# Starting offsets of SBUF buffers: low weights, mixing operands and large buffers placed within 256 bytes

## What is computed

```python
for l in range(2):
    x = x + 0.5 * swiglu(rmsnorm(x, ln_ffn1[l]), w_ffn1_gu[l], w_ffn1_down[l])
    h = rmsnorm(x, ln_mix[l])
    u_pool, q, k, v, gate_logits = split(h @ w_in[l])
    a = pool_mixer(u_pool, pool_w[l], pool_scale[l]) @ w_pool_branch[l]
    b = swa_sink_attention(rope(rmsnorm(q)), rope(rmsnorm(k)), v, sinks[l]) @ w_attn_branch[l]
    g_pool, g_attn = split(sigmoid(gate_logits))
    x = x + (g_pool * a + g_attn * b) @ w_out[l]
    x = x + 0.5 * swiglu(rmsnorm(x, ln_ffn2[l]), w_ffn2_gu[l], w_ffn2_down[l])
p = rmsnorm(x) @ w_in_2
x = x + concat(gated_delta_rule_both_ways(p), mlstm_both_ways(p)) @ w_out_2
x = x + peer(rmsnorm(x))     # top 16 of 128 x 128 experts in 8 heads, tables u and v
return rmsnorm(x)
```

## Time and profile before

| | |
|---|---|
| median of 3 runs | 4139.93 us (4137.62 to 4139.94) |
| profiled execution | 4135.88 us, span 4134.0 us |
| TensorE matmuls | busy 4077.5 us, 99% of the span, 19348 of them |
| weight loads | busy 3377.9 us (82%), beside the matmuls |
| VectorE, ScalarE, POOL | 48%, 35%, 46% busy |
| DMA | 486.47 MB, mean 118 GB/s |
| granted TensorE clock | 0.997 |

### The profile page before, as it was taken

How to read it: one execution, slowest core, us unless ns; L and a number is a source line. 1 busy time by engine, 2 the same in 40 slices (tenths; PEclk the granted TensorE clock), 3 DMA queues, 4 the chain that set the end, 5 groups by cost and what they waited for, 6 DMA issues and landing times.

```text
span 4134.0 us, 52711 instructions
## 1 busy us (share of the span) xinstructions
PE 4077.5 (99%) x19348; PEld 3377.9 (82%) x19348; DVE 1981.6 (48%) x3472; ACT 1455.7 (35%) x2192; POOL 1884.1 (46%) x1408
## 2 busy tenths in 40 slices
PE   9999999999999999999999999999999999999998
PEld 7888777888888877888777998888888888888887
DVE  3212553221220364321248453498788846666653
ACT  3222243222322234322324433333676632222222
POOL 4444334444444434444433534455433345555553
PEclk9999999999999999999999999999999999999999
DMA  3222122222222212222211002233455575555542
GB/s 133 100 101 95 72 72 92 91 102 91 94 99 102 93 63 82 92 91 102 98 72 41 1 11 103 94 144 132 174 205 204 203 249 185 191 203 193 185 170 82
DMA packets 134660, 486.47 MB, mean 118 GB/s; under 512 B 8704, under 2 KB 74496, under 8 KB 92032
## 3 DMA queue, kind: packets, MB, share of 16 engines
q1 hardware_dynamic: 49392, 351.29, 23.7%
q10 hardware_dynamic: 85136, 133.38, 9.3%
HBM read 417.54 MB, written 67.11 MB: 117 GB/s over the span
## 4 chain that ended last, share of the span: by engine, by line
PE 43%; issue 32%; POOL 21%; DVE 2%; ACT 1%; POOLq 0%; ACTq 0%; DVEq 0%
POOL w_lo L446 21%; PE bank L1139 12%; PE bank L1140 12%; PE bank L1141 12%; PE bank L1961 1%; PE bank L1714 1%; PE bank L1730 1%; PE bank L1726 1%; DVE gk L2374 0%; DVE gq L2374 0%; PE bank L1896 0%; DVE p_t L2385 0%; PE bank L1675 0%; PE bank L1573 0%; DVE p_t L2388 0%
## 5 line engine op out<-in xcount | busy, mean ns | idle before, releaser
L446 POOL TENSOR_TENSOR w_lo<-raw,w_hi 128x512 fp32r<-128x512 f32 x1324 | 1784.1, 1379 | 2118.5 <-ACT w_hi L554 2091.8
L1139 PE MATMUL bank<-h_hi,w_hi 128*128 128x512 f32 x3232 | 1271.6, 393 | 20.0 <-DVE h_lo L2088 9.8
L1140 PE MATMUL bank<-h_lo,w_hi 128*128 128x512 f32 x3232 | 1260.5, 390 | 0.0
L1141 PE MATMUL bank<-h_hi,w_lo 128*128 128x512 f32 x3232 | 1260.2, 390 | 0.0
L554 ACT ACTIVATE w_hi<-raw 128x2048 fp32r<-128x2048 f32 x331 | 633.1, 1913 | 1051.7 <-PE bank L1141 1017.9
L1139 PEld LDWEIGHTS bank<-h_hi,w_hi 128*128 128x128 f32 x3232 | 608.4, 188 | 152.3 <-POOL w_lo L446 16.3
L1141 PEld LDWEIGHTS bank<-h_hi,w_lo 128*128 128x128 f32 x3232 | 607.8, 188 | 128.2
L1140 PEld LDWEIGHTS bank<-h_lo,w_hi 128*128 128x128 f32 x3232 | 608.5, 188 | 123.7 <-issue 1.5
L1139 PE MATMUL bank<-w_mix_hi,w_hi 128*128 128x512 f32 x1024 | 398.4, 389 | 0.9 <-ACT stage L942 0.9
L1141 PE MATMUL bank<-w_mix_hi,w_lo 128*128 128x512 f32 x1024 | 398.3, 389 | 0.0
L1140 PE MATMUL bank<-w_mix_lo,w_hi 128*128 128x512 f32 x1024 | 398.3, 389 | 0.0
(11 more groups left out here) (378 smaller groups left out, 4463.4 us busy)
## 6 DMA issues: line engine op xcount, KB each, us to landing
raw<-weights SPq DMA_DIRECT2D x331, 1024.0 KB, 4.8
g_store<-g_buf ACTq DMA_DIRECT2D x8, 4096.0 KB, 18.2
g_in<-g_store ACTq DMA_DIRECT2D x32, 1024.0 KB, 5.5
s_store<-stage ACTq DMA_DIRECT2D x60, 512.0 KB, 2.9
s_in<-s_store ACTq DMA_DIRECT2D x30, 1024.0 KB, 7.5
x<-x_in SPq DMA_DIRECT2D x4, 512.0 KB, 8.0
out<-x SPq DMA_DIRECT2D x8, 256.0 KB, 2.2
keys_sb<-keys ACTq DMA_DIRECT2D x1, 1024.0 KB, 4.7
```

The costliest lines, as they stand in the source:

```text
L446: pool.tensor_tensor(w_lo[:, slot, cols], raw[:, slot, cols], w_hi[:, slot, cols].bitcast(F32), ALU.subtract).then_inc(lo_written, 1)
L1139: pe.matmul(out_ap, w_hi[:, slot, cols], m_hi, start=start, stop=False)
L1140: pe.matmul(out_ap, w_hi[:, slot, cols], m_lo, start=False, stop=False)
L1141: return pe.matmul(out_ap, w_lo[:, slot, cols], m_hi, start=False, stop=stop)
```

## The change

place gets an argument shift. A buffer of 2048 bytes a partition or more now begins at a multiple of LINE = 256 bytes plus shift, a smaller one at a multiple of 32 as before. Low weights are shifted by 64, att, y and mix_late by 64, y2 by 192; all other large buffers begin at 0 modulo 256. soft and headsel are placed earlier, among the small buffers, and a few buffers that lie over others are computed to the same rule. What moves, modulo 256: w_lo and a_t from 0 to 64; att, y and mix_late from 128 to 64; qk, v_tok, gates, pool_w_sb from 128 to 0; y2 from 224 to 192; const and the buffers of the delta rule and the mLSTM from 224 to 0, gv from 96 to 0. w_hi, raw, h, act, w_mix, hot_first and hot_parts stay at 0; act and w_mix move by 256 bytes. The highest byte used becomes 212,704. No instruction, wait or transfer is added or removed.

```diff
--- before.py
+++ after.py
@@ -114,6 +114,8 @@
 
 GATE_STEP = {"rows": 1, "read": 2, "logs": 3, "a": 4, "sums": 5, "m": 7, "floor": 8}
 
+LINE = 256
+
 
 def build(nc, x_in, weights, gains, small, pool_w, consts, rope, second, level_masks,
           keys, out):
@@ -123,11 +125,12 @@
         sizes = {F32: 4, F32R: 4, U32: 4}
         offset = [0]
 
-        def place(name, shape, dtype, at=None):
+        def place(name, shape, dtype, at=None, shift=0):
 
             nbytes = int(np.prod(shape[1:])) * sizes[dtype]
             if at is None:
-                at = offset[0]
+                step = LINE if nbytes >= 2048 else 32
+                at = -(-(offset[0] - shift) // step) * step + shift
                 offset[0] = -(-(at + nbytes) // 32) * 32
             return nc.alloc_sbuf_tensor_at(name, shape, dtype, offset=at + base)
 
@@ -147,20 +150,21 @@
         raw = place("raw", [P, 2, TILE * P], F32)
         w_hi_at = offset[0]
         w_hi = place("w_hi", [P, 2, TILE * P], F32R)
-        w_lo_at = offset[0]
-        w_lo = place("w_lo", [P, 2, TILE * P], F32R)
+        w_lo_at = offset[0] + LINE // 4
+        w_lo = place("w_lo", [P, 2, TILE * P], F32R, shift=LINE // 4)
+        soft = place("soft", [P, 2, 6, 4], F32)
         rstd = place("rstd", [P, TOKENS], F32)
-        sq_at = offset[0]
+        sq_at = -(-offset[0] // LINE) * LINE
         sq = place("sq", [P, 2, TOKENS], F32)
-        tmp_at = offset[0]
+        tmp_at = -(-offset[0] // LINE) * LINE
         tmp = place("tmp", [P, TOKENS], F32)
         rcol = place("rcol", [P, 3, TT], F32)
         gain = place("gain", [P, 9, KB], F32)
         small_sb = place("small_sb", [P, LAYERS, 14], F32)
+        headsel = place("headsel", [P, 2], F32)
         const = place("const", [P, 5, P], F32)
         mask = place("mask", [P, 2 * P], F32)
         invc = place("invc", [P, 4, PAD], F32)
-        headsel = place("headsel", [P, 2], F32)
         rope_sb = place("rope_sb", [P, 2, TOKENS], F32)
         region = offset[0]
         ident, swap, upper, lower, ones = (const[:, n, :] for n in range(5))
@@ -185,14 +189,13 @@
         probs_t0 = place("probs_t0", [P, 2, TOKENS], F32)
         gates = place("gates", [P, 2 * KB, TOKENS], F32)
 
-        mix_late = place("mix_late", [P, 4, 2, TOKENS], F32R, at=offset[0] - KB * TOKENS * 4)
-        att_hi = place("att_hi", [P, 4, TOKENS], F32R)
-        att_lo = place("att_lo", [P, 4, TOKENS], F32R)
-        y_hi = place("y_hi", [P, 4, TOKENS], F32R)
-        y_lo = place("y_lo", [P, 4, TOKENS], F32R)
+        mix_late = place("mix_late", [P, 4, 2, TOKENS], F32R, at=offset[0] + LINE // 4 - KB * TOKENS * 4)
+        att_hi = place("att_hi", [P, 4, TOKENS], F32R, shift=LINE // 4)
+        att_lo = place("att_lo", [P, 4, TOKENS], F32R, shift=LINE // 4)
+        y_hi = place("y_hi", [P, 4, TOKENS], F32R, shift=LINE // 4)
+        y_lo = place("y_lo", [P, 4, TOKENS], F32R, shift=LINE // 4)
         pool_w_sb = place("pool_w_sb", [P, 4, P], F32)
         rq = place("rq", [P, 3, TT, 10], F32)
-        soft = place("soft", [P, 2, 6, 4], F32)
 
 
         offset[0] = region
@@ -215,8 +218,9 @@
         head_gain = place("head_gain", [P, 8], F32)
         r3 = place("r3", [P, 3, TT, 8], F32)
         rn = place("rn", [P, 3, 32], F32)
-        m_row_at = offset[0]
-        m_row = place("m_row", [GH, 2, TOKENS], F32)
+        m_row_at = -(-offset[0] // LINE) * LINE
+        m_row = place("m_row", [GH, 2, TOKENS], F32, at=m_row_at)
+        offset[0] = m_row_at + 2 * TOKENS * 4
         head_squares = place("head_squares", [P, GH * P], F32, at=m_row_at)
         masks2 = place("masks2", [P, 9, P], F32)
         sq_second = place("sq_second", [P, KB, TOKENS], F32, at=offset[0])
@@ -256,8 +260,8 @@
                for p in range(2)]
         state = place("state", [P, 2, GH, P], F32, at=region - 2 * GH * P * 4)
         offset[0] = overlay
-        y2_hi = place("y2_hi", [P, KB, TOKENS], F32R)
-        y2_lo = place("y2_lo", [P, KB, TOKENS], F32R)
+        y2_hi = place("y2_hi", [P, KB, TOKENS], F32R, shift=3 * LINE // 4)
+        y2_lo = place("y2_lo", [P, KB, TOKENS], F32R, shift=3 * LINE // 4)
         a_row = tmp
```

## The result

The changed kernel takes **4192.74 us** (median of 4 runs, 4191.86 to 4193.27) against 4138.77 for the kernel before on the same chip, a ratio of 1.0133 [1.0121, 1.0146]. It is 54 us slower; the forecast was 4085, 54 us faster. The profiled run took 4193.27 us with a span of 4191.4, 57.4 us more than the 4134.0 of the earlier trace rows.

What follows compares the result with a forecast made beforehand. It took TensorE's matmul pace to bound the kernel. From the profiled 4135.9 us it took 50 for the low weights and 5 for mixing operands and y2, giving 4081, then 4 more for the runs' median: 4085, range 4036 to 4168.

Steps and rivals of the forecast that it cites:

- What bounds the kernel: TensorE, busy 4077.5 of 4134.0 us: only a change in the pace of its matmul stream can move the time much.
- Part 1: Low weights to 64, in 4960 triples with h, act and w_mix: 10 ns less each, 50 us gained.
- What is lost at the best place: Matmul stream with operands at 0: 12 to 13 ns lost at the start of each matmul, whatever its length.
- Part 2: Mixing operands from 128 to 64, y2 from 224 to 192, 960 matmuls: 5 us less.
- Part 3: Everything else to 0, touching two-pass matmuls, vector and POOL work: no change in time.
- Part 4: POOL writing low weights at 64: its work stays covered, 7.4 us beside 10.7 us of matmuls.
- Rival A: Low weights at 64 break the stream's even beat in each triple: 4165, or 4214 if whole triples slow; chance 0.2.
- Rival B: Weight loads stay hidden, so moving low weights does nothing; 0 to 6 us gained elsewhere, 4134 to 4140; chance 0.12.
- Rival C: The matmul after the changed load speeds up too: 20 to 25 ns a triple, 4036 down to 4011; chance 0.1.

Runs made afterwards that it cites:

- experiment 7: Separate program, not the kernel: 24 matmul stretches at varied widths and modes; for 512 columns float32r 226.7 ns, plain float32 215 a record, bf16 216.
- experiment 5: The changed kernel with low weights, mixing operands and y2 all at 0: 4133.61 us, ratio 0.9991 to the kernel before.
- experiment 2: The changed kernel with only the low weights back at 0: 4133.41 us, ratio 0.9991 to the kernel before.
- experiment 1: The kernel before with only the low weights moved to 64: 4193.67 us, ratio 1.014.
- the map: Separate program: 120 stretches of 20 float32r triples at varied operand and weight places, later 63 more in finer steps; fastest 680.0 ns a triple.

## Why the prediction was wrong

**What bounds the kernel** held: the time moved only through the pace of the matmul stream, and the 57.4 us are all in TensorE's busy time.

**Part 1, low weights at 64, failed**, in sign. It took a gain of 10 ns for each of 4960 triples from L1379 as the only row with the weights 64 ahead of the moving operand. Two things were wrong with that row. First, it is not at 64: a row of pool_u is PAD + TOKENS = 528 values, 2112 bytes, so only the first of its four products begins at 64, the others at 128, 192 and 0. The four, with weights at 128 each time, leave eight records, two a product and not one:

```profile
449.35 3.67 PE L1379 MATMUL bank<-pool_u,pool_w_sb 128*128 128x512 f32 x8 [0.41 <-issue]
```

From the second record on they start 429 or 430 ns apart, at all four distances; and L1311, 96 bytes apart, keeps the same step (its three records of the earlier trace rows in 1.45 us are two steps of 429 and one duration of 592). Second, L1379 is plain float32, and experiment 7 shows 215 ns a pass for that at no distance at all: what the row lacks, the mode lacks. The working named this ("it may be the two passes that hide the cost") and went by the distance all the same. Four rows of the same mode as the stream, 233 at 128, 233.5 at 224, 231.7 with 32 columns and 0.40 beside weights at 224, had all pointed to a loss. The last of them holds: with everything at 0 (experiment 5) the matmul in front of L1311's load has 389 ns where it had 396. The nearest row had to be chosen by mode first. Instead of -10 the term is +13.3 ns where the stream is dense and +10.7 in the mean for h. The upper bound of the term, +6 for one matmul, was also too low, because it priced only the matmul beside the load.

**What is lost at the best place** is 13.3 ns in float32r at 512 and 256 columns, as read, but not "whatever its length": experiment 7 has 16.7 at 504 and 58 at 128.

**Part 2** was right in sign and near in size: 5 us expected, about 3 found at the 2.4 GHz level; the run after hides them behind its two drops of the clock, and experiment 2 has 2.5 for parts 2 and 3 together. **Part 3** was right at nothing within that. **Part 4** was right: 13.0 us of waiting for POOL after, 14.4 before.

**Rival A** is what happened, between its two prices (4165 and 4214), and its words fit: the low weights throw the stream off its beat in each triple. It was to decide from 2 ns a triple, and 13.3 came. What it had missed is where: L1140's successor shows 392, not the 393 named as its sign, and most of the cost is on the matmul after it. It had 0.2, with four cases out of four for it; by its own account of the rows it deserved to be the forecast. **Rival B** fell with experiment 1: the Trainium skill, SBUF — State Buffer, "A bandwidth-pool intuition that's wrong (but worth ruling out)", has an independent port for weights, and this case does not bear out that the two streams are therefore independent in time: on the map, 0; 64, 64 takes 700.0 ns and all at 64 680.0, with nothing changed but where weights lie against the moving operand. **Rival C** fell with the maps: nothing tried is below 680.

The range, 4036 to 4168, missed by 25 us, as it took in only the milder half of A.

## What to carry to other kernels

In a dense stream of float32r matmuls, let both halves of the weights and of the moving operand begin at the same offset modulo 256 bytes; which one it is did not matter here, and 64 bytes of difference in one of four operands cost this kernel 1.3%. Borrow a price only from rows of the same matmul mode, work out the address of every product of the row and not of the first alone, and where several rows of that mode agree against one of another, go with them. An effect of addresses is cheap to measure: one small program maps a hundred settings before anything in the kernel is moved. Average such a stretch over whole repeats of its pattern: a few matmuls more or less moved one price from 693.3 to 691.8 and a forecast by 8 us.

## What the runs showed of the hardware

- The pace of a float32r matmul of 512 columns at the 2.4 GHz level is 226.7 ns with equal offsets and up to 240 (distance 120); bf16 makes 216 at three places of its weights.
- 8 bytes of distance already cost 20 ns a triple (680.0 to 700.0). So in these runs the effect doesn't follow units of 16, 64 or 256 bytes, although it repeats modulo 256.
- A distance costs time on matmuls beside which nothing changed: behind the moved weights' product the step is 235.8, beside their load 229.2. Why it falls there is open.
- The means of triples often lie 6.67 ns apart (680.0, 686.7, 693.3, 700.0), and the steps between starts repeat as a fixed sequence, over four triples with the low weights at 192. The distances do not fix the sequence wholly: two settings settled at different paces with the same distances (700.0 and 686.7, 693.3 and 700.0). What in the chip has this step, and why 144 and 240 are free for the low weights alone, no run here tells.
- Plain float32 shows no price for distance: L1379's records stay 429 or 430 ns apart at four distances.
- The fastest versions, all operands at 0 or all at 64, are 4.5 and 3.5 us under the kernel before, with intervals that reach no change (0.9982 to 1.0 and 0.9982 to 1.0001).
